# Two-block transformer kernel on one Trainium2 core: 28 weight blocks of each block's input projection on split operands, another order of the first stage, convolution sums in PSUM

## The reference, cut to what matters

```python
# first block
h = modulate(rms_norm(x, norm1_g), sh1, sc1)
u = h @ w_in                       # query, key/value, 2048 convolution columns, 2048 gate columns
y = a * sigmoid(g)                 # GLU on the convolution columns (a, g = halves)
y = depthwise_conv(y, 31 taps) + conv_b
y = silu(layer_norm(y)) @ w_pw
g = sigmoid(u[..., OFF_GATE:])
x = x + g1 * ((g_a * attention_out + g_c * y) @ w_out)
...                                # then a product-key expert layer
# second block
proj = rmsnorm(x, ln1_g) @ w_in_2  # 5632 columns
y_sb = stick_breaking_attention(q_sb, k_sb, v_sb)
o = hgrn2_chunk_scan(silu(q_hg), 1 - f, log(f), i_hg)
...                                # gates, merge, mixture of experts
```

## Time and profile before

| | |
|---|---|
| median of 3 runs | 1756.51 us (1756.34 to 1758.08) |
| the profiled execution | 1755.58 us, span 1753.8 us |
| busy: TensorE / VectorE / ScalarE / GpSimd | 1707.7 / 1016.7 / 676.0 / 341.0 us |
| the chain of work that ended last | TensorE 92%, VectorE 3%, transfers 3%, ScalarE 1% |
| granted TensorE clock | 0.993 of full |

### The profile page before, as it was taken

One profiled execution on the slowest core, in us unless ns is written; L12 is line 12 of the kernel. 1 busy time (PEld: TensorE's weight loads), 2 busy tenths in 40 slices (PEclk: granted clock), 3 DMA queues, 4 the chain that ended last, 5 costly groups with the idle time before them and its releaser, 6 DMA issues.

```text
span 1753.8 us, 24837 instructions
## 1 busy us (share of the span) xinstructions
PE 1707.7 (97%) x9466; PEld 1354.1 (77%) x9466; DVE 1016.7 (58%) x2037; ACT 676.0 (39%) x956; POOL 341.0 (19%) x175
## 2 busy tenths in 40 slices
PE   7999999999999999999999999999999999899997
PEld 4878766879999999777788888888877888655454
DVE  2679565630995888877776776677423642422113
ACT  2111364434445566433345555445346130221212
POOL 1010000647786999120000000000000000000000
PEclk9999999999999999999999999999999999999999
DMA  9466421334543222455555555556522326599995
GB/s 387 153 230 250 168 96 49 125 140 160 199 174 140 73 97 91 174 188 186 194 175 190 183 182 189 188 191 224 234 87 105 116 104 268 195 426 428 428 428 224
DMA packets 33344, 343.73 MB, mean 196 GB/s; under 512 B 3952, under 2 KB 4592, under 8 KB 5360
## 3 DMA queue, kind: packets, MB, share of 16 engines
q1 hardware_dynamic: 31968, 339.78, 51.3%
q10 hardware_dynamic: 1296, 2.84, 0.4%
HBM read 340.51 MB, written 2.10 MB: 195 GB/s over the span
## 4 chain that ended last, share of the span: by engine, by line
PE 92%; DVE 3%; DMA 3%; ACT 1%; issue 1%; SPq 0%; DVEq 0%; PEldq 0%
PE psD L623 25%; PE psY L951 20%; PE psD L803 8%; PE psD L937 6%; PE psD L1175 5%; PE psY L911 5%; PE psD L808 4%; PE psD L927 3%; PE psD L939 3%; PE psD L1184 3%; DMA arena<-in_experts 2%; PE psY L775 2%; PE psY L659 1%; DMA ring<-in_w_mod 1%; PE psY L623 1%; PE psD L790 1%
## 5 line engine op out<-in xcount | busy, mean ns | idle before, releaser
L951 PE MATMUL psY<-ring_r,work_r 128*128 128x512 f32 x1536 | 365.9, 393 | 1.8 <-issue 1.8
L951 PEld LDWEIGHTS psY<-ring_r,work_r 128*128 128x128 f32 x1536 | 280.1, 188 | 71.7 <-issue 10.7
L1298 ACT ACTIVATE arena<-psD 128x512 f32<-128x512 f32 (+5 forms) x182 | 124.8, 689 | 434.4 <-PE psD L623 230.1
L1298 ACT ACTIVATE ring_r<-ring 128x1024 fp32r<-128x1024 f32 x188 | 192.7, 1056 | 170.0 <-PE psY L951 115.2
L623 PE MATMUL psD<-xh,ring 128*128 128x256 f32 x1024 | 230.1, 384 | 2.6 <-DVE xh L1830 1.3
L623 PEld LDWEIGHTS psD<-xh,ring 128*128 128x128 f32 x1024 | 194.3, 192 | 36.5 <-issue 8.8
L937 PE MATMUL psD<-xh_r,ring_r 128*128 128x512 f32 x480 | 171.3, 397 | 0.0
L2106 DVE TENSOR_TENSOR ring_r<-ring,ring_r 128x1024 fp32r<-128x1024 f32 x128 | 156.3, 1221 | 14.6 <-ACT ring_r L1298 14.3
L1744 POOL TENSOR_TENSOR ring_r<-ring,work_r 128x1024 fp32r<-128x1024 f32 x48 | 116.7, 2438 | 244.1 <-ACT work_r L1298 244.1
L939 PE MATMUL psD<-xh_r,ring_r 128*128 128x256 f32 x480 | 134.6, 280 | 0.0
L937 PEld LDWEIGHTS psD<-xh_r,ring_r 128*128 128x128 f32 x480 | 90.2, 188 | 21.6
(11 more groups left out here) (347 smaller groups left out, 2774.0 us busy)
## 6 DMA issues: line engine op xcount, KB each, us to landing
ring<-in_tables SPq DMA_DIRECT2D x60, 1024.0 KB, 4.9
arena<-in_experts SPq DMA_DIRECT2D x30, 2048.0 KB, 19.7
ring<-in_w_in SPq DMA_DIRECT2D x18, 2048.0 KB, 9.1
ring<-in_experts SPq DMA_DIRECT2D x18, 2048.0 KB, 18.0
ring<-in_early_v SPq DMA_DIRECT2D x34, 1024.0 KB, 4.9
ring<-in_w_mod SPq DMA_DIRECT2D x12, 2048.0 KB, 8.7
ring<-in_early_u SPq DMA_DIRECT2D x11, 2048.0 KB, 8.4
ring<-in_mid_u SPq DMA_DIRECT2D x12, 1024.0 KB, 4.9
```

The source lines that it names most:

```text
L951: last = nc.tensor.matmul(psY[:, t * D + h * 512:t * D + (h + 1) * 512], wgt[:, b, t * P:(t + 1) * P], v[:, h * 512:(h + 1) * 512], start= ...
L1298: return nc.scalar.activation(dst, src, f, **kw)
```

## The change

1. Seven of the eight loads of the first stage (14 pairs, 28 blocks; all but the first GLU load) go through `split`. ScalarE rounds the activations once (`h1_hi`, 8 pieces) and each weight block (28 rounds); GpSimd makes the lo parts. Rounds run three to four blocks ahead: after each pair's result is taken, ScalarE rounds two more.
2. The list `FIRST` changes: the third GLU load now stands before the first gate load.
3. The two sums of the convolution lie in PSUM (`cacc = aux(3)`), all but the last value of one, which goes to SBUF. Modulation parts 5 and up then share one bank.
4. The copy of the rotary keys (`kr_spread`) moves on GpSimd from before the weight splits to behind the 28 of them.
5. In the second block the pairs p0 to p3 and p6 to p15 (28 blocks) go through `split` in the same way; VectorE's decay weights read `El` and `cum_wide`, which lie in PSUM now; after the scan one copy of 128x1024 fills `cum_wide`. ScalarE copies the lo part of the activations (128x2048) to another place after p5.

```diff
-FIRST = [("glu", 0), ("glu", 2), ("gate", 0), ("glu", 4), ("gate", 2), ("glu", 6), ("gate", 4), ("gate", 6)]
+FIRST = [("glu", 0), ("glu", 2), ("glu", 4), ("gate", 0), ("glu", 6), ("gate", 2), ("gate", 4), ("gate", 6)]
...
+            def split_product(ps, hi, lo, n, x_hi, x_lo, frees=0, after=None):
+                pe.wait_ge(u_hi_ready, n)
+                for k in range(K):
+                    if after:
+                        pe.wait_ge(after[0], after[1] + k + 1)
+                    for i, x in enumerate((x_hi, x_lo)):
+                        last = nc.tensor.matmul(ps, hi[:, k * P:(k + 1) * P], x[:, k, :], start=(k + i == 0), stop=False)
...
+                pe.wait_ge(u_lo_ready, n)
+                for k in range(K):
+                    last = nc.tensor.matmul(ps, lo[:, k * P:(k + 1) * P], x_hi[:, k, :], start=False, stop=(k == K - 1))
...
-                    wt = use(first_block(2 * FIRST.index((kind, n - n % 2))))
-                    pair(TILE[f"{kind}{n}"], wt, 2 * (n % 2), hT, 1 - n % 2, (h_ready, 0) if (kind, n) == ("glu", 0) else None)
+                    i = FIRST.index((kind, n - n % 2))
+                    if i == 0:
+                        pair(TILE[f"{kind}{n}"], use(first_block(0)), 2 * n, hT, 1 - n, None if n else (h_ready, 0))
+                    else:
+                        ps = tile(TILE[f"{kind}{n}"])
+                        for j in range(2):
+                            c = 4 * (i - 1) + 2 * (n % 2) + j
+                            last = split(ps[:, j * T:(j + 1) * T], c, c + 1, h1_hi, h1_lo, ...)
...
+            def first_ahead(i, half):
+                q = 2 * (i - 1) + half
+                for c in (2 * q + 3, 2 * q + 4):
+                    if c < SPLIT_IN:
+                        weight_round(c)
...
                 elif kind == "gate":
                     ps = take(TILE[f"gate{m}"])
                     fn(flat(gates[:, 2 * m:2 * m + 2, :]), ps[:, :], ACT.Sigmoid).then_inc(tile_free["act"], 1)
+                    first_ahead(FIRST.index((kind, m - m % 2)), m % 2)
...
+            cacc = aux(3).rearrange("p (a t) -> p a t", a=2)
...
-                    s[j % 2] = mark(stt(acc, y[:, j:j + T], conv_w[:, m * TAPS + j:m * TAPS + j + 1], acc,
-                                        ALU.mult, ALU.add))
+                    s[j % 2] = mark(stt(cpart if j == TAPS - 2 else acc, y[:, j:j + T],
+                                        conv_w[:, m * TAPS + j:m * TAPS + j + 1], acc, ALU.mult, ALU.add))
...
+                if c == SPLIT_IN:
+                    pool.wait_ge(u_lo_ready, c)
+                    pool.wait_ge(krope_ready, 1)
...
+            def second_pair(i, n):
+                ps = tile(i)
+                if n in (0, 6):
+                    pe.wait_ge(h_split, 4 * K)
+                    pe.wait_ge(h_hi_ready, 4 * K + (n > 0))
+                for j in range(2):
+                    d = 2 * SPLIT2.index(n) + j
+                    last = split_product(ps[:, j * T:(j + 1) * T], hi2(d), split2_at(ring_r, d), U2 + d + 1, h2_hi, ...)
...
-        El, Dl = ar(18688, 4, T), ar(19712, 4, T)
+        Dl = ar(19712, 4, T)
+        El, cum_wide = (psY[:, i * 1024:(i + 1) * 1024].rearrange("p (k t) -> p k t", k=4) for i in range(2))
```

More of the change, by code:

```diff
@@ L47 @@
 CANDS = 72
-SPLIT_O, SPLIT_OUT, SPLIT_PQ = 8, 6, 14
-SPLITS = SPLIT_O + SPLIT_OUT + SPLIT_PQ
+SPLIT_IN, SPLIT_O, SPLIT_OUT, SPLIT_PQ = 28, 8, 6, 14
+AT_O = SPLIT_IN
+AT_OUT = AT_O + SPLIT_O
+AT_PQ = AT_OUT + SPLIT_OUT
+SPLITS = AT_PQ + SPLIT_PQ
+SPLIT2 = [p for p in range(16) if p // 2 != 2]
 ROWS = [(0, 1, 16), (1, 4, 8), (4, 8, 4), (8, 16, 2)]
@@ L289, in ar, with wk @@
             return v
-        def wk(at, n, x1=False):
-            return (pick[:].rearrange("p a t -> p (a t)") if x1 else work)[:, at:at + n]
+        def wk(at, n, aside=False):
+            if aside and at == 1024:
+                return ar(30976, n)
+            return (pick[:].rearrange("p a t -> p (a t)") if aside else work)[:, at:at + n]
         hcT, sq, cxn, ctxT = ar(0, K, T), ar(2048, K, T), ar(4096, K, T), ar(16384, K, T)
@@ L792, in _ @@
                     last.then_inc(tile_ready, 1)
-            def split(ps, c, n, x_hi, x_lo, frees=0, after=None):
-                hi, lo = top_hi[c % 3], split_at(ring_r, c)
-                pe.wait_ge(u_hi_ready, n)
-                for k in range(K):
-                    if after:
-                        pe.wait_ge(after, k + 1)
-                    for i, x in enumerate((x_hi, x_lo)):
-                        last = nc.tensor.matmul(ps, hi[:, k * P:(k + 1) * P], x[:, k, :], start=(k + i == 0), stop=False)
-                        if k + i == 0 and frees:
-                            last.then_inc(w_used, frees)
-                pe.wait_ge(u_lo_ready, n)
-                for k in range(K):
-                    last = nc.tensor.matmul(ps, lo[:, k * P:(k + 1) * P], x_hi[:, k, :], start=False, stop=(k == K - 1))
-                    if k == 0:
-                        last.then_inc(split_done, 1)
-                return last
             def plain(ps, wt, f, src, after, step, frees):
@@ L1371, in _ @@
                     fn(flat(cq), ps[:, :], ACT.Copy).then_inc(tile_free["act"], 1)
+                    act.wait_ge(ctx_norm_ready, 1)
+                    for k in range(K):
+                        act.wait_ge(h_ready, k + 1)
+                        fn(h1_hi[:, k, :], hT[:, k, :], ACT.Copy).then_inc(h_hi_ready, 1)
                 elif kind == "u":
                     kv_out(TILE["u1"], 0)
+                    for c in range(3):
+                        weight_round(c)
                 elif kind == "ctx":
@@ L1594, in _, with round2, round_ahead @@
             root(at=T)
+            for k in range(K):
+                act.wait_ge(h_part, K + k + 1)
+                fn(h2_hi[:, k, :], hT[:, k, :], ACT.Copy).then_inc(h_hi_ready, 1)
+            def round2(d):
+                idx = STREAM["w_in2"] + 1 + SPLIT2[d // 2] // 2
+                act.wait_ge(w_loaded[idx % RING], 16 * (idx // RING + 1))
+                if d >= 3:
+                    act.wait_ge(split_done, S2 + d - 2)
+                fn(hi2(d), split2_at(ring, d), ACT.Copy).then_inc(u_hi_ready, 1)
+            def round_ahead(n):
+                for d in (2 * SPLIT2.index(n) + 3, 2 * SPLIT2.index(n) + 4):
+                    if d < 2 * len(SPLIT2):
+                        round2(d)
+            for d in range(3):
+                round2(d)
             for t in range(TT):
@@ L2251, in weights @@
                 elif level == 7:
[L2252 to L2253 removed]
+                    u, v, d = (flat(x).rearrange("p (n s b) -> p n s b", s=2, b=CHUNK) for x in (cum, cum_wide, Dl))
+                    mark(tt(d[:, :, 0, :], u[:, :, 0, CHUNK - 1:CHUNK].broadcast_to([P, 8, CHUNK]), v[:, :, 0, :],
                             ALU.subtract))
@@ L2606, in pack @@
         experts[p, 4 + side] = cols(a("w_exp_down_2")[0, e], D)[0]
+    tiled = {3 + p // 2 for p in SPLIT2}
     lb = a("hg_lb_logits_2")
@@ L2624, in pack @@
         "early_u": early_u, "mid_u": mid_u, "early_v": early_v, "tables": tables,
-        "w_in2": cols(a("w_in_2")[0]),
+        "w_in2": np.concatenate([tiles(a("w_in_2")[0][:, i * 512:(i + 1) * 512]) if i in tiled else
+                                 cols(a("w_in_2")[0][:, i * 512:(i + 1) * 512]) for i in range(11)]),
         "w_bsb": cols(a("w_branch_sb_2")[0], D)[0],
```

150 lines of the change are left out of this document (101 added, 49 removed).

## The result

The changed kernel takes 1764.73 us (median of 5 runs, 1763.71 to 1766.11) against 1756.34 (5 runs). The ratio is 1.0046, with a 95% interval of 1.0033 to 1.006, so it is slower. The forecast was 1757.9, so the time is 6.8 us above it. It is inside the range of 1748 to 1767 that was given for 8 in 10, but outside the forecast's own 1754 to 1762 and on the other side of the bound of 0.2%: of my cases the one called "slower" came out.

What follows compares the result with a forecast made beforehand. TensorE held 92% of the chain, with VectorE only 2.4 us behind in the first stage. First stage +13.2, heads -3.0, levels -8.75 gave +1.4 us, so 1757.9 for the median; own range 1754 to 1762, 8 in 10 1748 to 1767.

Steps and rivals of the forecast that it cites:

- The restart of VectorE: First stage: the root behind gate pair 1 ends at 122.9, so VectorE restarts 11.4 us later than before.
- The taps: Convolution sums in PSUM: opening taps cost +0.2 a piece, +1.0 us in all; the 29 others keep their rate.
- rival 3: Slower: convolution taps with a PSUM sum lose their overlap, +0.08 us each, +12, so 1770; chance 0.07.
- Operations with two SBUF inputs behind GpSimd: Convolution's GLU products and norms wait for GpSimd's weight splits, one or two of eight: +1.5 us, bounds 0 and 11.6.
- rival 1: Slower: GpSimd's splits hold all eight GLU products and norms, 1.45 us each, +10, so 1768; chance 0.14.
- The last pair and the clock: From "mean" on: 1.1 us less for the shorter last gate pair, +2.8 for TensorE's half clock after idling.
- The heads: Second block, eight heads up to level 1: ScalarE takes half of the gain, leaving -3.0 us, bounds 0 and -7.5.
- three heads in which TensorE waits for ScalarE: Second block: in three heads with sigmoid, log and silu (table load 1.3, 1.06 us each), ScalarE delays TensorE.
- The levels: Second block behind the heads: 7 pairs save 1.25 us each, -8.75 us, bounds -4 and -10.
- All stay under TensorE: Second block's levels: ScalarE (3.8 of 7.9 us), GpSimd (4.9) and VectorE never hold up TensorE.
- Rival 2: Slower: second block gives nothing in heads, half in levels, as lo parts come late: -4, so 1765.5; chance 0.14.
- Rival 4: Faster: TensorE's saving arrives as root or load comes sooner, no clock lost, p0 and heads give all: 1750; chance 0.20.

Runs made afterwards that it cites:

- e1: The changed kernel with the old list FIRST (third GLU load behind the first gate load): 1749.99 us, ratio 0.9962.
- e2: The changed kernel, new order kept, with the two roots of the query and key/value norms earlier on ScalarE: 1737.31 us, ratio 0.9886.
- e4: The changed kernel with the three norm operations behind piece 7 of the convolution instead of piece 5: 1761.32 us, ratio 1.0029.
- e7: The changed kernel with early roots, norms behind piece 7, lo copy on GpSimd and the second block's silu three levels sooner: 1736.19 us, ratio 0.9891.
- e10: The changed kernel with 12 unread matmuls of 128x512 on TensorE in its idle time ahead of "mean": 1763.98 us, ratio 1.0039.
- e6: The changed kernel with the second block's copy of the activations' lo part on GpSimd instead of ScalarE: 1764.63 us, ratio 1.005.
- e12: As e7, but with the norms behind the subtraction of the mean, without unread matmuls: 1734.98 us, ratio 0.9867.

## Why the prediction was right in its mechanism and 7 us short in size

The path moved to VectorE, by the wait that was named; what it put too small is the price of GpSimd's splits on VectorE's operations, and in the second block two waits on ScalarE.

- **A split pair.** 5.76 us were taken. Gate pairs 0 and 1 took 11.69 us from the start of the first to the start of what follows them (103.72 to 115.41): 5.85 each. Right within 0.1.
- **The restart of VectorE.** 122.9 was forecast, 122.94 measured; e1 and e2 show that the root's place is the cause. As a sum it was right by two errors that cancel: TensorE was 2.5 us ahead of the trace of before when the split pairs began (the clock at the start, below), and the load of block 12 took 13.51 us, not 11.5.
- **The taps.** The opening taps cost +0.25 a piece and the 29 behind them -0.11, together +0.14 instead of +0.2. Right. A tap takes 0.396 us against 0.400, which refutes rival 3. The rule of the Trainium skill ("VectorE: DVE Perf Modes", section on the TRN2 errata) with its 120 cycles for a source in PSUM is not seen here either.
- **Operations with two SBUF inputs behind GpSimd: the term that failed.** Taken +1.5, measured +5.7: the norms +4.67 (6.13 us from the first to the next product, 1.46 before), two products +1.03. The bound of 11.6 held. I counted one or two of eight meetings from the gaps in GpSimd's work; it was five, at 1.1 us each on average. GpSimd's splits come in twos and threes after a load, and the norms fell into the middle of three. This is rival 1 at four tenths of its size (4.2 of 10), and e4 and e7 show that moving an operation changes which one is caught, so the number of meetings could not be had from averages.
- **"mean".** 200.25 instead of 196.45. The difference of 3.8 is the term above (4.2), less 0.3 for the taps.
- **The last pair and the clock.** +1.7 forecast, +1.63 measured; e10 gives the clock's part as 2.5 where I had 2.8.
- **The heads.** -3.0 forecast, -1.87 measured. p1 waits for z1 (1.56 us) as said. The step that failed is "three heads in which TensorE waits for ScalarE": TensorE waited 0.96 us ahead of p6 for the copy of 1.90 us, 0.81 and 0.92 in p7 and 1.69 at the first level. With the copy on GpSimd (e6) the heads give -3.43 in the trace.
- **The levels.** -8.75 forecast, -6.59 measured. The pitch is right (7.97 for 7.9). "All stay under TensorE" failed at the last level, where ScalarE's silu and sigmoid now end behind the point where p14 has to be taken: the pair was done at 1432.06 and taken at 1433.89. In e7 the silu stands three levels sooner, this wait is gone and the block is 1.15 us shorter than in e6.
- **The sum.** Forecast +1.4. The profiled pair gave +8.35, 6.95 more: GpSimd 4.2, levels 2.2 and heads 1.1 make 7.5, and the taps and the stretch between the blocks give 0.6 back.

Rival 2 went less than half of its way (the block gave -8.46 instead of -11.75, not -4). Rival 4 named the true remedy, a root that comes sooner, but for the wrong kernel: it was not in the change. Its sum has a slip: -8 on 1756.5 (1755.58 and the 0.9 of the median) gives 1748.5, not 1750.

## What to carry to other kernels

When a split or a faster format frees one engine, find out what the engine that follows it waits for, and move that first: here the place of two roots in ScalarE's order decided between +8 and -20 us. An operation that another engine's burst holds up has to be costed by its place in the burst, not by the burst's average share, and every move upstream changes the place. An edit that is worth nothing alone (early roots in the kernel before) can be the larger part of a pair.

## What the runs showed of the hardware that was not expected

TensorE's clock differs between executions at the same place, where TensorE's work is the same up to there. Stretches of both traces (us, busy (x) of PE, PEld, DVE, ACT, POOL, clock, DMA share, GB/s), before and after:

```profile
36.00:40.00 4.00, 3.45 (x8) 2.85 (x9) 3.20 (x9) 0.00 (x0) 1.19 (x1) 0.50 1.02 344
```

```profile
36.00:40.00 4.00, 3.38 (x16) 3.02 (x17) 3.24 (x10) 0.00 (x0) 1.11 (x1) 1.00 1.00 360
```

The same 64 records behind it took 16.60 us in the profile of before, 14.05 in that of after, and 14.05 to 17.09 in the others, whichever kernel it was. One trace set against another is uncertain by up to 3 us for that alone.

The price of "mean" behind a long idle time varies as well, and not with the length of the idle time: to the next piece it took 6.13 us behind 12.78 us without work (e1), 4.75 behind 20.77 (e4) and 5.88 behind 26.27 (the changed kernel). And a wait of 1.9 to 2.2 us ahead of "mean" was enough for a stretch at 1.2 GHz (e2, e7, e12: 5.04 to 5.06 us from "mean" to the next piece instead of 3.45), while the same place filled with two unread matmuls stayed at 2.4 GHz (3.37 us).
